# Both block compressions side by side on TensorE, the head factors between them, gate sums and first attention scores after them

## The chip, the cores and the metric

One Trainium2 chip, one core of it. The metric is the device time of one execution in microseconds (us). The kernel before takes 2090.16 us, the median of three runs (2089.99, 2090.16 and 2095.55).

## The reference: what is computed

One inference step of a decoder trunk with two layers, for a prompt of 512 tokens and for 8 sequences with 4 new tokens each (544 columns in all). Each layer has two token mixers, an mLSTM (matrix memory, 4 heads) and a sparse attention (8 query heads, 2 key heads), whose outputs are gated and merged, and then a SwiGLU channel mixer. The part that the change touches:

```
def compress(raw, pe, w1, w2):
    ...
    blocks = jnp.concatenate([ch[:, :-1], ch[:, 1:]], axis=2) + pe[None, None, :, None, :]
    hid = jax.nn.gelu(jnp.einsum('bnlgd,lde->bnge', blocks, w1))
    return jnp.einsum('bnge,ef->bngf', hid, w2)
...
kc = compress(k_cmp, pe_k, w1_k, w2_k)
vc = compress(v_cmp, pe_v, w1_v, w2_v)
...
h = h * lax.rsqrt(jnp.mean(h * h, axis=-1, keepdims=True) + EPS) * norm_g.astype(jnp.float32).reshape(M_HEADS, M_HEAD_DIM)
out = h.reshape(B, T, M_WIDTH) * jax.nn.sigmoid(o.astype(jnp.float32))
...
out = g[..., 0:1] * o_c + g[..., 1:2] * o_s + g[..., 2:3] * o_w
```

The attention has three branches: over compressed keys and values (`kc`, `vc`), over selected blocks, and over a window. Each has a softmax and a gate.

## The kernel before, in words

Each engine runs one list of instructions per layer, in the order in which its function is written (`tensor_layer`, `scalar_layer`, `vector_layer`, `gpsimd_layer`, `sync_layer`), and engines wait for one another by semaphores. No scheduler moves anything: what stands later in a function waits behind what stands earlier on that engine.

A layer goes: norm, input products, mLSTM, then the stretch of this change, then attention in 38 steps, then the large products (line 834, over half of TensorE's instructions). The stretch between mLSTM and attention, in TensorE's order:

1. `compress(0)` (lines 1178 to 1189, keys): 64 products of 64 rows by 161 columns, 16 for each of four weight units `w1`. It writes banks 0 and 6 of the result memory `ps` (`HIDDEN_BANK`). In the trace each product is two instructions, so 128.
2. The head factors (line 1203): for each of the four heads, a matrix of 4 rows spreads that head's factor over 128 partitions. The first two heads go at once. The third waits for the first one's `ha_ready`, the fourth for the second one's, since they write the same two banks. VectorE multiplies each head's output by its factor and by its sigmoid gate (lines 1812 and 1814) and signals `ha_ready`.
3. The gate sums (line 1209): the gates of the new tokens are spread into rows of `ps`. VectorE turns them into `gsel` (lines 1829 and 1830).
4. The scores of attention steps 0 and 1 (`att_scores`, line 1081), after all four `ha_ready`.
5. `compress(1)` (values), which waits for `gs_read`, VectorE's signal that the gate sums are read.
6. The second products of both compressions (lines 1222 to 1226), each behind ScalarE's `hid_ready` (GELU, lines 1510 to 1513); then ScalarE copies the compressed keys and values out (lines 1515 to 1517) and signals `cmp_ready`.
7. The scores of step 2 (line 1078), then the loop over steps: `att_turn(k)` (transposes, line 1100), the scores of step k + 3, `att_out(k)`.

ScalarE's order there is: `ha_high` of each head (line 1503, a rounding copy that is the upper half of a split; VectorE makes the lower half in line 1893), the exponentials of steps 0 and 1 (`att_exp`, line 1471), the scaling of step 0 (`att_scale`, line 1481), then both GELUs, the three copies, and the exponentials of step 2. VectorE's is: head factors, small copies of the new tokens' queries (line 1822), gate sums, masks and maxima of steps 0 and 1 (lines 1851 and 1854), weights of step 0, the four lower halves, weights of step 1 together with mask and maximum of step 2, and so on. `att_turn(1)` needs ScalarE's scaling of step 1, which comes after its exponentials of step 2.

The weight units are loaded by SyncE into a ring of four slots; a unit of `compress(1)` is loaded once the same quarter of `compress(0)` is done (`w1_used`).

Of the kernel before, what the change touches and what calls it, by code (L numbers as in the profile page):

```python
# [9 lines left out]
ALU = mybir.AluOpType  # L10
# [4 lines left out]
AX = mybir.AxisListType  # L15

P = 128
# [67 lines left out]
def columns(spec):  # L85
    at, out = 0, {}
    for name, width in spec:
# [51 lines left out]
             "cs_done": 4, "c_decayed": 4, "kw_summed": 3, "pc_done": 1, "rope_ready": 6, "hid_ready": 2,  # L139
             "cmp_done": 1, "cmp_ready": 1, "qb_ready": 1, "s_done": 38, "max_ready": 38, "exp_done": 38, "weight_ready": 30,  # L140
             "p_ready": 30, "cp_ready": 8, "t_done": 58, "t_free0": 29, "t_free1": 29, "o_done": 58, "hb_ready": 6,
             "gs_done": 1, "gs_read": 1, "merged_ready": 8, "qb_cleared": 1, "c0_landed0": 32, "c0_landed1": 32,
             "page_landed0": 64, "page_landed1": 64, "page_landed2": 64, "page_landed3": 64}

def build_step(nc, xT_in, W_in, small_in, const_in, c0_in, pages_in, table_in, win_in, cwin_in,
               y_out, fm_out, raw_out, knew_out, tm_out, u_out, pC_out, pn_out, m_out, sC_out, oldwin_out):
    with ExitStack() as ctx:
        def sb(name, shape, dt=F32):
            return ctx.enter_context(nc.sbuf_tensor(name, shape, dt))

        def sem(name):
            return ctx.enter_context(nc.semaphore(name))

        def since(layer, s, n):

            return layer * PER_LAYER[s.name] + n

        def group(layer, key):

            return layer * len(GROUPS) + GROUP[key]  # L160
# [61 lines left out]
        nstat = sb("nstat", [P, MH, 1 + DECB])  # L222
        gsel = sb("gsel", [P, 2, 3])
        gtmp = sb("gtmp", [P, 3, NH])
        hbias = sb("hbias", [P, 2])
        table = sb("table", [1, DECB * NPG], I32)
        big = slab[:, MIX_AT:SLAB_W]
# [96 lines left out]
        def bc(ap, shape):  # L324
            return ap.to_broadcast(shape)
# [95 lines left out]
        t_free = [sem(f"t_free{s}") for s in range(2)]  # L421
        o_done = sem("o_done")
        hb_ready = sem("hb_ready")
        gs_done = sem("gs_done")
        gs_read = sem("gs_read")
        merged_ready = sem("merged_ready")
        dve_step = sem("dve_step")
# [342 lines left out]
        def tensor_layer(pe, layer):  # L770
# [12 lines left out]
            def drained(q):  # L783

                for s in range(4):
                    pe.wait_ge(pair_free[s], (q - s + 3) // 4)
# [388 lines left out]
                pe.wait_ge(so_copied, since(layer, so_copied, hb + 1))  # L1175
                pe.transpose(ps[:, 7, P:2 * P], so[:, hb, :], ident).then_inc(so_turned, 1)

            def compress(v):
                for u in range(4):
                    w = landed(("w1", 4 * v + u)).rearrange("p (l e) -> p l e", e=HID)  # L1180
                    for l8 in range(8):
                        l = 8 * u + l8
                        second, l16 = divmod(l, STRIDE)
                        for g in range(NKV):

                            x = raw[g * HD:(g + 1) * HD, v, l16, second:second + NBLK + 1]
                            mm = pe.matmul(ps[:, HIDDEN_BANK[v][g], 0:NBLK + 1], w[g * HD:(g + 1) * HD, l8, :], x,  # L1187
                                           start=(l == 0), stop=(l == CLEN - 1))
                    mm.then_inc(w1_used, 1)
# [5 lines left out]
            compress(0)  # L1195
            read_out(layer, pe, ("rope", 3))
            read_out(layer, pe, ("k", 1))
            pe.wait_ge(scale_ready, since(layer, scale_ready, 1))
            for h in range(MH):
                if h >= 2:  # L1200
                    pe.wait_ge(ha_ready, since(layer, ha_ready, h - 1))
                for a in range(2):
                    mm = pe.matmul(ps[:, 2 + 2 * (h % 2) + a, 0:NHALF], sel4[0:MH, h, :], scales[:, a * NHALF:(a + 1) * NHALF],
                                   start=True, stop=True)
                mm.then_inc(scale_done, 1)
            drained(group(layer, ("ga", 0)))

            for hb in range(2):
                mm = pe.matmul(ps[:, 7, hb * 24:(hb + 1) * 24], tsel[0:NS, hb, :], gate[0:NS, TT, :], start=True, stop=True)
            mm.then_inc(gs_done, 1)  # L1210

            pe.wait_ge(rope_ready, since(layer, rope_ready, 6))
            pe.wait_ge(q_moved, since(layer, q_moved, 1))
            pe.wait_ge(ha_ready, since(layer, ha_ready, MH))
            att_scores(0)
            att_scores(1)
            pe.wait_ge(gs_read, since(layer, gs_read, 1))
            compress(1)
            w2 = sml("w2", "p (v f) -> p v f", v=2)
            pe.wait_ge(hid_ready, since(layer, hid_ready, 1))  # L1220
            for g in range(NKV):
                pe.matmul(ps[g * HD:(g + 1) * HD, 0, 0:NBLK], w2[:, 0, :], hid[:, 0, g, :], start=True, stop=True)
            pe.wait_ge(hid_ready, since(layer, hid_ready, 2))
            for g in range(NKV):
                pe.matmul(ps[0:NCP, 5, g * HD:(g + 1) * HD], hid[:, 1, g, 0:NCP], w2[:, 1, :], start=True, stop=True)
                mm = pe.matmul(ps[:, 5, P + g * HD:P + (g + 1) * HD], hid[:, 1, g, PBLK:NBLK], w2[:, 1, :], start=True, stop=True)
# [42 lines left out]
        def scalar_layer(act, layer):  # L1269
# [196 lines left out]
            def att_exp(k):  # L1466
                act.wait_ge(max_ready, since(layer, max_ready, k + 1))
                if before(k) is not None:
                    act.wait_ge(t_done, since(layer, t_done, pieces_through(before(k))))
                for r in range(parts_of(k)):  # L1470
                    ins = act.activation(part(prob(k), k, r), part(score(k), k, r), ACT.Exp, bias=stat[:, k % 3, r:r + 1],  # L1471
                                         accum_out=stat[:, 3 + k % 3, r:r + 1] if own_total(k) else None)
                ins.then_inc(exp_done, 1)
# [24 lines left out]
                            ins = act.copy(d[:, b4], o[:, b4, kv])  # L1498
                    ins.then_inc(hb_ready, 1)

            for h in range(MH):
                act.wait_ge(ha_ready, since(layer, ha_ready, h + 1))
                act.copy(ha_high[h], haT[:, h, :]).then_inc(ha_high_ready, 1)
            att_exp(0)
            att_exp(1)
            att_scale(0)

            for v in range(2):
                act.wait_ge(w1_used, since(layer, w1_used, 4 * (v + 1)))
                link(act.copy(hbias[:, v:v + 1], ps[:, HIDDEN_BANK[v][0], NBLK:NBLK + 1]))  # L1510
# [3 lines left out]
            act.wait_ge(cmp_done, since(layer, cmp_done, 1))  # L1514
            act.copy(kcT, ps[:, 0, 0:NBLK])
            act.copy(vcp[0:NCP, :], ps[0:NCP, 5, 0:P])
            act.copy(vcs, ps[:, 5, P:2 * P]).then_inc(cmp_ready, 1)

            att_exp(2)
            for k in range(NSTEP):  # L1520
# [54 lines left out]
        def vector_layer(dve, layer):  # L1575
            steps = dve_steps

            def link(ins):

                steps[0] += 1  # L1580
                ins.then_inc(dve_step, 1)
                dve.wait_ge(dve_step, steps[0])
# [225 lines left out]
            dve.wait_ge(o_gated, since(layer, o_gated, 1))  # L1808
            for h in range(MH):
                dve.wait_ge(scale_done, since(layer, scale_done, h + 1))  # L1810
                by = ps[:, 2 + 2 * (h % 2):4 + 2 * (h % 2), 0:NHALF]
                link(dve.scalar_tensor_tensor(out=halves(qm[:, h, :]), in0=halves(qm[:, h, :]), scalar=sml("mng")[:, h:h + 1], in1=by,
                                              op0=ALU.mult, op1=ALU.mult))
                dve.tensor_tensor(haT[:, h, :], haT[:, h, :], qm[:, h, :], ALU.mult).then_inc(ha_ready, 1)
# [7 lines left out]
                        ins = dve.tensor_copy(qb[g * HD:(g + 1) * HD, a, :, g * 16 + r * 4:g * 16 + r * 4 + 4],  # L1822
                                              per_seq(src[g * HD:(g + 1) * HD, r, SEQ:N]))
            ins.then_inc(qb_ready, 1)

            dve.wait_ge(gs_done, since(layer, gs_done, 1))
            for hb in range(2):
                gall = ps[:, 7, hb * 24:(hb + 1) * 24].rearrange("p (h b) -> p b h", b=3)
                link(dve.tensor_tensor(gtmp[:, :, :], gall, bc(con("rowm").unsqueeze(1), [P, 3, NH]), ALU.mult))
                ins = dve.tensor_reduce(gsel[:, hb, :], gtmp[:, :, :], AX.X, ALU.add)  # L1830
                link(ins) if hb == 0 else ins.then_inc(gs_read, 1)

            def mask_of(k):

# [52 lines left out]

            weight_and_max(None, 0)
            weight_and_max(None, 1)
            weight_and_max(0, None)  # L1890
            for h in range(MH):
                dve.wait_ge(ha_high_ready, since(layer, ha_high_ready, h + 1))
# [343 lines left out]
```

## Time and profile before

| | |
|---|---|
| median of three runs | 2090.16 us |
| the profiled execution | 2090.03 us |
| its span in the trace | 2088.4 us |
| TensorE matmul busy | 1976.9 us, 95% of the span |
| VectorE busy | 984.3 us, 47% |
| ScalarE busy | 676.0 us, 32% |
| mean granted TensorE clock | 0.952 of full speed |

Times inside the trace are us from the start of the span. The first layer's stretch starts at 273.5, the second layer's at 1305.2. A start and a duration stand ahead of each piece; "x128" is the number of instructions merged in one row. The granted clock is 1.00 for 2.4 GHz and 0.50 for 1.2 GHz; a value between is a stretch with both.

### The profile page before, as it was taken

The numbers are of one execution on the slowest core, as the hardware profiler recorded it, in microseconds if no ns is written. First come the engines' busy times: TensorE is split into PE (matmuls) and PEld (weight loads), VectorE is DVE, ScalarE is ACT, GpSimd is POOL, SyncE is SP. The second block draws the span as 40 slices with busy tenths as digits, with TensorE's granted clock in tenths as the row PEclk, the third lists the DMA queues.
The fourth block names the chain that finished last, engine by engine and source line by source line (L and its number), as shares of the span: only waits on it lengthen the run. The fifth ranks groups of instructions, "written<-read, shape, count | busy, mean of one in ns | idle before, by whom it ended". The sixth has DMA issues, their size and how long they took to land.

```text
span 2088.4 us, 34564 instructions
## 1 busy us (share of the span) xinstructions
PE 1976.9 (95%) x14490; PEld 1794.6 (86%) x14490; DVE 984.3 (47%) x1688; ACT 676.0 (32%) x1315; POOL 106.6 (5%) x148
## 2 busy tenths in 40 slices
PE   6999988889999999999989999988899999999997
PEld 5878875569999999999977878645799999999996
DVE  6343655733345442444363355666333554424434
ACT  4523236742223221222235223467322332212221
POOL 0011212000000000000001122100000000000000
PEclk9989987989999999999989899889899999999998
DMA  4202233012222223222131113520222222222221
GB/s 180 100 21 77 98 109 139 1 51 92 85 88 91 82 91 105 82 91 92 61 113 42 46 61 102 158 77 2 71 92 91 82 91 86 87 92 86 87 91 44
DMA packets 47531, 174.18 MB, mean 83 GB/s; under 512 B 6442, under 2 KB 6474, under 8 KB 46930
## 3 DMA queue, kind: packets, MB, share of 16 engines
q1 hardware_dynamic: 40178, 142.71, 21.1%
q0 software_dynamic: 7200, 29.27, 4.1%
q8 instruction: 116, 1.90, 0.4%
q14 instruction: 37, 0.30, 0.0%
HBM read 161.37 MB, written 14.71 MB: 84 GB/s over the span
## 4 chain that ended last, share of the span: by engine, by line
PE 86%; DVE 7%; ACT 5%; issue 2%; DMA 0%; DVEq 0%; SPq 0%; ACTq 0%; POOLq 0%
PE ps L834 59%; PE ps L796 3%; ACT slab L1471 2%; PE ps L1008 2%; PE ps L1187 2%; DVE stat L1854 2%; PE ps L1009 2%; PE ps L1010 2%; PE ps L872 1%; PE ps L874 1%; PE ps L873 1%; PE ps L1100 1%; PE ps L949 1%; ACT slab L1481 1%; PE ps L1081 1%
## 5 line engine op out<-in xcount | busy, mean ns | idle before, releaser
L834 PE MATMUL ps<-xh,late_w 128*128 128x272 f32 x3840 | 645.7, 289 | 1.8 <-ACT slab L1498 1.8
L834 PEld LDWEIGHTS ps<-xh,late_w 128*128 128x128 f32 x3840 | 545.1, 189 | 2.6 <-issue 2.3
L1603 DVE TENSOR_TENSOR late_w<-ring,late_w 128x1024 fp32r<-128x1024 f32 x196 | 240.2, 1225 | 645.7 <-ACT late_w L1300 645.7
L1300 ACT CAST late_w<-ring 128x1024 fp32r<-128x1024 f32 x196 | 205.3, 1048 | 716.5 <-PE ps L834 716.4
L834 PE MATMUL ps<-xl,late_w 128*128 128x272 f32 x1920 | 397.5, 289 | 0.0
L834 PEld LDWEIGHTS ps<-xl,late_w 128*128 128x128 f32 x1920 | 303.4, 190 | 0.0
L834 PE MATMUL ps<-ah,late_w 128*128 128x272 f32 x1408 | 234.7, 288 | 0.0
L834 PEld LDWEIGHTS ps<-ah,late_w 128*128 128x128 f32 x1408 | 198.7, 188 | 0.0
L1471 ACT ACTIVATE slab<-ps,stat 128x31 f32<-128x31 f32 (+5 forms) x204 | 84.4, 450 | 84.4 <-DVE stat L1854 84.4
L834 PE MATMUL ps<-mh,late_w 128*128 128x272 f32 x576 | 98.9, 288 | 0.0
L1008 PE MATMUL ps<-xh,fill_w 128*128 128x272 f32 x256 | 86.1, 336 | 0.8
L834 PEld LDWEIGHTS ps<-mh,late_w 128*128 128x128 f32 x576 | 82.3, 188 | 0.1
L1118 PEld LDWEIGHTS ps<-slab,vkv 128*64 128x64 f32 x640 | 36.2, 145 | 52.7 <-DVE slab L1905 24.9
L834 PE MATMUL ps<-al_first,late_w 128*128 128x272 f32 x384 | 79.3, 288 | 0.0
L1009 PE MATMUL ps<-xl,fill_w 128*128 128x272 f32 x256 | 78.2, 305 | 0.0
L1010 PE MATMUL ps<-xh,fill_w 128*128 128x272 f32 x256 | 77.8, 304 | 0.0
L1100 PE MATMUL ps<-const,slab 128*128 128x128 f32 (+1 forms) x384 | 62.8, 306 | 12.6 <-ACT slab L1481 12.6
L796 PE MATMUL ps<-slab,ring 128*128 128x272 f32 x256 | 63.7, 414 | 10.7 <-DVE slab L1615 10.7
L1481 ACT ACTIVATE slab<-slab,stat 128x128 f32<-128x128 f32 (+4 forms) x140 | 68.9, 558 | 10.1 <-DVE stat L1877 10.0
L796 PEld LDWEIGHTS ps<-slab,ring 128*128 128x128 f32 x256 | 51.5, 202 | 23.6 <-issue 12.2
L1100 PEld LDWEIGHTS ps<-const,slab 128*128 128x128 f32 (+1 forms) x384 | 45.2, 149 | 30.4 <-ACT slab L1481 21.5
L1118 PE MATMUL ps<-slab,vkv 128*64 128x128 f32 x640 | 54.7, 300 | 16.8 <-ACT slab L1532 9.1
(328 smaller groups left out, 2997.5 us busy)
## 6 DMA issues: line engine op xcount, KB each, us to landing
ring<-in_W SPq DMA_DIRECT2D x258, 512.0 KB, 3.5
slab<-in_pages POOLq DMA_DIRECT2D x64, 128.0 KB, 2.5
slab<-in_c POOLq DMA_DIRECT2D x8, 512.0 KB, 4.4
out_sC<-slab POOLq DMA_DIRECT2D x8, 512.0 KB, 3.1
slab<-in_win POOLq DMA_DIRECT2D x2, 2048.0 KB, 8.0
out_oldwin<-in_cwin POOLq DMA_DIRECT2D x2, 2016.0 KB, 14.1
xT<-in_xT SPq DMA_DIRECT2D x8, 272.0 KB, 4.5
out_y<-slab SPq DMA_DIRECT2D x8, 272.0 KB, 2.1
```

Of the source, the lines that this page charges most:

```text
L796: mm = pe.matmul(out[:, a, :], w[:, k, :], src[:, k, a * NHALF:(a + 1) * NHALF], start=(k == 0), stop=(k == kcs - 1))
L834: mm = pe.matmul(out[:, a, :], w[:, k * P:(k + 1) * P], x[:, a * NHALF:(a + 1) * NHALF], start=start, stop=stop)
L1008: pe.matmul(ps[:, 5, 0:NHALF], wh[:, w], xh[:, c, cols], start=(c == 0), stop=False)
L1009: pe.matmul(ps[:, 5, 0:NHALF], wh[:, w], xl[:, c, cols], start=False, stop=False)
L1010: mm = pe.matmul(ps[:, 5, 0:NHALF], wl[:, w], xh[:, c, cols], start=False, stop=(c == KC - 1))
L1100: mm = pe.transpose(ps[0:rows, 5 + x % 2, at:at + P], piece, ident)
L1118: mm = pe.matmul(ps[hd(kv), 7, r0 * P:(r0 + 1) * P], vkv[:, j, (br - 1) * P + kv * HD:(br - 1) * P + (kv + 1) * HD], PT[:, x % 2, (2 * c + ...
L1187: mm = pe.matmul(ps[:, HIDDEN_BANK[v][g], 0:NBLK + 1], w[g * HD:(g + 1) * HD, l8, :], x, start=(l == 0), stop=(l == CLEN - 1))
L1300: act.copy(hi, ring[:, u % RING, 0:hi.shape[1]]).then_inc(wh_ready, 1)
L1471: ins = act.activation(part(prob(k), k, r), part(score(k), k, r), ACT.Exp, bias=stat[:, k % 3, r:r + 1], accum_out=stat[:, 3 + k % 3, r:r ...
L1481: ins = act.activation(part(prob(k), k, r), part(prob(k), k, r), ACT.Copy, scale=stat[:, 8 + k % 3, r:r + 1])
L1603: dve.tensor_tensor(lo, ring[:, u % RING, 0:hi.shape[1]], hi.bitcast(F32), ALU.subtract).then_inc(wl_ready, 1)
```

## The change

TensorE: `compress` takes the units that it is to do. After `compress(0)` come the factors of heads 0 and 1, units 0 and 1 of `compress(1)`, the factors of heads 2 and 3, units 2 and 3 of `compress(1)`, and then the scores of steps 0 and 1. The factors use banks 1 to 4 in place of 2 to 5, since `compress(1)` writes banks 5 and 7. The gate sums move between the second products and go to unused columns of bank 5; no wait for `gs_read` is left on TensorE. ScalarE: GELUs and copies come first, with one new copy (`gall`, the gate sums, out of `ps`), then the exponentials of steps 0 and 1 and the scaling of step 0, then the four `ha_high`. VectorE: the reduction of the gate sums reads the copy and stands behind the maxima of steps 0 and 1, after `cmp_ready`.

```
-            def compress(v):
-                for u in range(4):
+            def compress(v, units=range(4)):
+                for u in units:
...
-            pe.wait_ge(scale_ready, since(layer, scale_ready, 1))
-            for h in range(MH):
+            drained(group(layer, ("ga", 0)))
+
+            def head_scales(h):
+
                 if h >= 2:
                     pe.wait_ge(ha_ready, since(layer, ha_ready, h - 1))
                 for a in range(2):
-                    mm = pe.matmul(ps[:, 2 + 2 * (h % 2) + a, 0:NHALF], ...
+                    mm = pe.matmul(ps[:, 1 + 2 * (h % 2) + a, 0:NHALF], ...
                 mm.then_inc(scale_done, 1)
-            drained(group(layer, ("ga", 0)))
-
-            for hb in range(2):
-                mm = pe.matmul(ps[:, 7, hb * 24:(hb + 1) * 24], tsel[0:NS, hb, :], gate[0:NS, TT, :], start=True, stop=True)
-            mm.then_inc(gs_done, 1)
+
+            pe.wait_ge(scale_ready, since(layer, scale_ready, 1))
+            head_scales(0)
+            head_scales(1)
+            compress(1, (0, 1))
+            head_scales(2)
+            head_scales(3)
+            compress(1, (2, 3))
...
             att_scores(0)
             att_scores(1)
-            pe.wait_ge(gs_read, since(layer, gs_read, 1))
-            compress(1)
...
             pe.wait_ge(hid_ready, since(layer, hid_ready, 2))
+            for hb in range(2):
+                pe.matmul(ps[:, 5, (2 + hb) * P:(2 + hb) * P + 24], tsel[0:NS, hb, :], gate[0:NS, TT, :], start=True, stop=True)
...
-            for h in range(MH):
-                act.wait_ge(ha_ready, since(layer, ha_ready, h + 1))
-                act.copy(ha_high[h], haT[:, h, :]).then_inc(ha_high_ready, 1)
-            att_exp(0)
-            att_exp(1)
-            att_scale(0)
-
+            act.wait_ge(ha_ready, since(layer, ha_ready, MH))
             for v in range(2):
...
             act.copy(vcp[0:NCP, :], ps[0:NCP, 5, 0:P])
+            act.copy(gall[:, :, :], ps[:, 5, 2 * P:4 * P].rearrange("p (a n) -> p a n", a=2)[:, :, 0:3 * NH])
             act.copy(vcs, ps[:, 5, P:2 * P]).then_inc(cmp_ready, 1)
+
+            att_exp(0)
+            att_exp(1)
+            att_scale(0)
+            for h in range(MH):
+                act.copy(ha_high[h], haT[:, h, :]).then_inc(ha_high_ready, 1)
...
             weight_and_max(None, 0)
             weight_and_max(None, 1)
+            dve.wait_ge(cmp_ready, since(layer, cmp_ready, 1))
+            for hb in range(2):
+                link(dve.tensor_tensor(gtmp[:, :, :], gall[:, hb, :].rearrange("p (h b) -> p b h", b=3),
+                                       bc(con("rowm").unsqueeze(1), [P, 3, NH]), ALU.mult))
...
             weight_and_max(0, None)
```

TensorE, from the first compression to the first transposes; the piece of the difference (rows count products, not the trace's instructions; L1187 is the compression in both kernels, L1203 and L1205 the head factors, L1209 and L1228 the gate sums, L1081 the first scores):

```order
 L1187 MATMUL ps<-slab,ring 128x161 x64
-L1203 MATMUL ps<-slab,const 128x272 x8
-L1209 MATMUL ps<-gate,const 128x24 x2
+L1205 MATMUL ps<-slab,const 128x272 x4
+L1187 MATMUL ps<-slab,ring 128x161 x32
+L1205 MATMUL ps<-slab,const 128x272 x4
+L1187 MATMUL ps<-slab,ring 128x161 x32
 L1081 MATMUL ps<-slab 128x256 x4
-L1187 MATMUL ps<-slab,ring 128x161 x64
-L1222 MATMUL ps<-slab,small 64x160 x2
```

The second compression now stands in two halves ahead of the scores, and nothing of VectorE's work except two heads' `ha_ready` is waited for in between.

ScalarE, the same place, before (L1503 is `ha_high`, L1471 and L1481 exponentials and scaling, L1510 and L1512 the GELU with its bias, L1515 to L1517 the copies out):

```order
L1503 CAST sq_high<-slab 128x544 x2
L1503 CAST rstd_high<-slab 128x544
L1503 CAST acc_high<-slab 128x544
L1471 ACT_TABLE_LOAD
L1471 ACTIVATE slab,stat<-ps,stat 128x128 x8
L1481 ACTIVATE slab<-slab,stat 128x128 x4
L1510 COPY hbias<-ps 128x1
L1512 ACT_TABLE_LOAD
L1512 ACTIVATE slab<-ps,hbias 128x160 x2
...
L1517 COPY slab<-ps 128x128
L1471 ACT_TABLE_LOAD
L1471 ACTIVATE slab<-ps,stat 128x31 x4
```

ScalarE in the changed kernel (L1509 and L1511 the GELU, L1514 to L1517 the copies, L1476 and L1486 exponentials and scaling, L1523 `ha_high`):

```order
L1509 COPY hbias<-ps 128x1
L1511 ACT_TABLE_LOAD
L1511 ACTIVATE slab<-ps,hbias 128x160 x2
...
L1516 COPY gall<-ps 128x48
L1517 COPY slab<-ps 128x128
L1476 ACT_TABLE_LOAD
L1476 ACTIVATE slab,stat<-ps,stat 128x128 x8
L1486 ACTIVATE slab<-slab,stat 128x128 x4
L1523 CAST sq_high<-slab 128x544 x2
L1523 CAST rstd_high<-slab 128x544
L1523 CAST acc_high<-slab 128x544
L1476 ACTIVATE slab<-ps,stat 128x31 x4
```

The eight exponentials, the four scalings and the four `ha_high` now stand between the last copy out and the exponentials of step 2 (the four of 128x31); one table load fewer is left.

## Rows read from the trace of the kernel before

**Rows 1.** The page's chain that ended last: shares of the span by line.

```profile
PE ps L834 59%; PE ps L796 3%; ACT slab L1471 2%; PE ps L1008 2%; PE ps L1187 2%; DVE stat L1854 2%; PE ps L1009 2%; PE ps L1010 2%; PE ps L872 1%; PE ps L874 1%; PE ps L873 1%; PE ps L1100 1%; PE ps L949 1%; ACT slab L1481 1%; PE ps L1081 1%
```

**Rows 2.** Chain of waits in layer 0: start, duration, engine, line, instructions.

```profile
273.50 9.05 PE ps L1187 x128
...
293.55 9.96 PE ps L1187 x128
...
304.45 0.30 PE ps L1225 x2
...
305.75 0.29 ACT slab L1515
...
307.51 0.31 DVE ps L1851
...
310.47 1.12 PE ps L1100 x4
```

**Rows 3.** Timeline between the two compressions, layer 0: start, duration, engine, line, instructions.

```profile
282.48 2.10 PE L1203 MATMUL ps<-slab,const 4*128 4x272 f32 x8
...
285.35 0.64 ACT L1503 CAST sq_high<-slab 128x544 fp32r<-128x544 f32 x1 [12.36 <-DVE slab L1814]
285.37 3.99 PE L1203 MATMUL ps<-slab,const 4*128 4x272 f32 x8 [0.79 <-DVE slab L1814]
...
288.71 1.21 PEld L1209 LDWEIGHTS ps<-gate,const 32*128 32x128 f32 x4
...
289.40 0.78 DVE L1812 SCALAR_TENSOR_TENSOR slab<-slab,small,ps 128x544 f32<-128x544 f32 x1 [0.28 <-PE ps L1203]
290.22 0.72 DVE L1814 TENSOR_TENSOR slab<-slab 128x544 f32<-128x544 f32 x1
```

**Rows 4.** Timeline from the second compression's start to the first transposes, layer 0.

```profile
294.86 0.37 ACT L1471 ACTIVATE slab<-ps,stat 128x128 f32<-128x128 f32 x1 [1.93 <-DVE stat L1854]
...
297.61 1.30 ACT L1481 ACTIVATE slab<-slab,stat 128x128 f32<-128x128 f32 x4
...
298.79 0.72 DVE L1893 TENSOR_TENSOR ha_low<-slab,acc_high 128x544 fp32r<-128x544 f32 x1
...
303.41 0.49 PE L1222 MATMUL ps<-slab,small 128*64 128x160 f32 x4
...
306.09 0.25 ACT L1517 COPY slab<-ps 128x128 f32<-128x128 f32 x1
...
306.36 1.28 ACT L1471 ACT_TABLE_LOAD   x1
...
307.99 0.70 PE L1081 MATMUL ps<-slab 64*128 64x256 f32 x4
```

**Rows 5.** Windows: stretch, length, busy PE, PEld, DVE, ACT, POOL, granted clock, DMA share, GB/s.

```profile
282.50:284.60 2.10, 2.08 (x10) 1.38 (x8) 0.79 (x2) 0.00 (x0) 0.00 (x0) 1.00 0.78 252
285.00:285.25 0.25, 0.00 (x0) 0.00 (x0) 0.25 (x2) 0.00 (x0) 0.00 (x0) 0.85 0.69 279
295.25:295.50 0.25, 0.25 (x6) 0.25 (x4) 0.22 (x2) 0.25 (x3) 0.00 (x0) 0.67 0.00 0
310.50:321.50 11.00, 11.00 (x40) 6.17 (x40) 6.57 (x21) 6.09 (x28) 4.40 (x9) 0.50 0.73 263
```

**Rows 6.** Chain of waits in layer 1: first compression, first transposes of step 1.

```profile
1305.22 9.05 PE ps L1187 x128
...
1341.15 0.90 PE ps L1100 x3
```

**Rows 7.** Timeline: the first large product after attention, layers 0 and 1.

```profile
447.43 0.79 PE L834 MATMUL ps<-xh,late_w 128*128 128x272 f32 x2 [0.91 <-ACT slab L1498]
...
1479.04 0.80 PE L834 MATMUL ps<-xh,late_w 128*128 128x272 f32 x2 [0.91 <-ACT slab L1498]
```

**Rows 8.** The second compression's loads: the timeline's row of SyncE, the page's DMA issues.

```profile
276.00 23.47 SPq L632 DMA_DIRECT2D ring<-in_W  x6
...
ring<-in_W SPq DMA_DIRECT2D x258, 512.0 KB, 3.5
```

More of the change, by code:

```diff
@@ L141 @@
              "p_ready": 30, "cp_ready": 8, "t_done": 58, "t_free0": 29, "t_free1": 29, "o_done": 58, "hb_ready": 6,
-             "gs_done": 1, "gs_read": 1, "merged_ready": 8, "qb_cleared": 1, "c0_landed0": 32, "c0_landed1": 32,
+              "gs_read": 1, "merged_ready": 8, "qb_cleared": 1, "c0_landed0": 32, "c0_landed1": 32,
              "page_landed0": 64, "page_landed1": 64, "page_landed2": 64, "page_landed3": 64}
@@ L224, in build_step @@
         gtmp = sb("gtmp", [P, 3, NH])
+        gall = sb("gall", [P, 2, 3 * NH])
         hbias = sb("hbias", [P, 2])
@@ L423, in build_step @@
         hb_ready = sem("hb_ready")
-        gs_done = sem("gs_done")
         gs_read = sem("gs_read")
@@ L1202, in tensor_layer @@
                 for a in range(2):
-                    mm = pe.matmul(ps[:, 2 + 2 * (h % 2) + a, 0:NHALF], sel4[0:MH, h, :], scales[:, a * NHALF:(a + 1) * NHALF],
+                    mm = pe.matmul(ps[:, 1 + 2 * (h % 2) + a, 0:NHALF], sel4[0:MH, h, :], scales[:, a * NHALF:(a + 1) * NHALF],
                                    start=True, stop=True)
                 mm.then_inc(scale_done, 1)
-            drained(group(layer, ("ga", 0)))
-            for hb in range(2):
-                mm = pe.matmul(ps[:, 7, hb * 24:(hb + 1) * 24], tsel[0:NS, hb, :], gate[0:NS, TT, :], start=True, stop=True)
-            mm.then_inc(gs_done, 1)
+            pe.wait_ge(scale_ready, since(layer, scale_ready, 1))
[5 more added lines that the diff above has]
+            compress(1, (2, 3))
             pe.wait_ge(rope_ready, since(layer, rope_ready, 6))
@@ L1810, in vector_layer @@
                 dve.wait_ge(scale_done, since(layer, scale_done, h + 1))
-                by = ps[:, 2 + 2 * (h % 2):4 + 2 * (h % 2), 0:NHALF]
+                by = ps[:, 1 + 2 * (h % 2):3 + 2 * (h % 2), 0:NHALF]
                 link(dve.scalar_tensor_tensor(out=halves(qm[:, h, :]), in0=halves(qm[:, h, :]), scalar=sml("mng")[:, h:h + 1], in1=by,
@@ L1824, in vector_layer @@
             ins.then_inc(qb_ready, 1)
[L1826 to L1831, printed above, removed]
             def mask_of(k):
@@ L1889, in vector_layer @@
             weight_and_max(None, 1)
+            dve.wait_ge(cmp_ready, since(layer, cmp_ready, 1))
+            for hb in range(2):
+                link(dve.tensor_tensor(gtmp[:, :, :], gall[:, hb, :].rearrange("p (h b) -> p b h", b=3),
+                                       bc(con("rowm").unsqueeze(1), [P, 3, NH]), ALU.mult))
+                ins = dve.tensor_reduce(gsel[:, hb, :], gtmp[:, :, :], AX.X, ALU.add)
+                link(ins) if hb == 0 else ins.then_inc(gs_read, 1)
             weight_and_max(0, None)
```

## The prediction

> **What bounds the kernel now.** I read the page's chain first: it is TensorE's, and most of it lies in the large products, which the change leaves alone [rows 1]. So only two stretches matter, one per layer, from the first compression to the moment at which attention runs as before. For these I read the chain of waits, then the timeline row by row, then the granted clock.
>
> The marks in layer 0 are [rows 2]: the first compression from 273.50 for 9.05 us, the second from 293.55 to 303.51, the copies out from 305.75, the mask of step 2 at 307.51, the transposes of step 1 at 310.47. I call that last moment "turn 1". From there each step of attention follows the one before as in the changed kernel, since neither the order nor the work behind it changes. So the whole change is worth the difference in the distance from the first compression's start to turn 1: 310.47 - 273.50 = 36.97 us in layer 0, and 1341.15 - 1305.22 = 35.93 us in layer 1 [rows 2, 6].
>
> Two things are to be seen. Between the compressions TensorE spends 293.55 - 282.55 = 11.0 us on little work, waiting for VectorE's head multiplications, and part of it at 1.2 GHz: eight instructions of head factors take 2.10 us, the next eight 3.99 us [rows 3]. And while the second compression runs, ScalarE does the exponentials of steps 0 and 1 (from 294.86) and the scaling (from 297.61), and VectorE ends the lower halves (298.79), all before the compression ends [rows 4]. That work is free there. The change closes the first hole and takes the cover off the second.
>
> **The new distance, part by part** (us after the first compression's start, the same for both layers).
>
> *TensorE up to the values.* Two compressions at the first one's pace: 2 x 9.05 = 18.1. Two pairs of head factors: 2.10 each in the row, including the drain of the last one [rows 3]; an estimate is 1.95 where the next matmuls follow at once, 3.9 together. Sum 22.0. No wait arises: heads 2 and 3 need heads 0 and 1 multiplied, two times 0.78 + 0.72 us [rows 3], and 4.5 us of compression lie before. The weights do not hold it up either: the first unit of the second compression is issued at 276.00 and a unit lands in 3.5 us [rows 8], while it is needed at about 284.5; the last is issued as the first compression ends and needed some 11 us later. The multiplications of heads 2 and 3 (3.0 us) and the GELU of the keys with its table load (1.28, the size of the load in [rows 4]) run beside the last 4.5 us of compression.
>
> Then the scores of steps 0 and 1: four instructions are 0.70 [rows 4], eight I put at 1.1, so 23.1. The GELU of the values ends before that: in the old kernel the first value product starts at 304.45, 0.94 after the compression's end [rows 2]. Second products of the keys 0.49 [rows 4], less drain 0.4: 23.5. The gate sums are four weight loads, 1.21 at 1.2 GHz [rows 3], so half of it, 0.6, at 2.4 GHz: 24.1. Value products, 304.45 to the copies at 305.75 [rows 2]: 1.3, so 25.4. The copies up to the end of the last one (306.09 + 0.25 = 306.34, [rows 4]) are 0.6; the new copy of the gate sums adds at most the 0.25 of that last row, I take 0.2. The compressed keys and values are ready at **26.2**. Before it was 306.34 - 273.50 = 32.84 in layer 0. Up to here the change saves 6.6 us.
>
> *From there to turn 1.* Before: 310.47 - 306.34 = 4.13. Now ScalarE has its list in front of step 2, one after another: table load 1.28, eight exponentials from 294.86 to 297.61 = 2.75, scaling 1.30 [rows 4], four upper halves at 0.64 = 2.6 [rows 3]. VectorE's last lower half follows with 0.72 [rows 4], and only then comes the mask of step 2, because weights of step 1 and mask of step 2 stand behind the lower halves in VectorE's order. From the mask to turn 1 it is 310.47 - 307.51 = 2.96 as before [rows 2]. Sum 1.28 + 2.75 + 1.30 + 2.6 + 0.72 + 2.96 = **11.6**. The scores of step 2 on TensorE and VectorE's reduction of the gate sums lie beside this list. The cover of all this was the second compression, and it is gone.
>
> *Sum.* 26.2 + 11.6 = 37.8. Against 36.97 that is +0.8 us in layer 0, against 35.93 it is +1.9 us in layer 1: +2.7 us. The profiled execution took 2090.03 us, so **2092.7 us**; that execution lies 0.1 us from the median shown. It is +0.13%, and 0.3% (6.3 us) is about what a measurement of this kernel can tell from no change.
>
> *Bounds of the unknown sizes.* Upper: head factors at 2.10, scores at twice 0.70, keys at 0.49, new copy at 0.25: +0.7 per layer. Lower: gate sums hidden in neighbouring loads (-0.6) and the scaling and halves overlapping by 0.1 per instruction of the halves (-0.4): -1.0 per layer. GpSimd's output and page loads start some 8 us earlier; I cost them at nothing, since no row here has TensorE waiting on them. After turn 1 the same instructions took 447.43 - 310.47 = 136.96 us in layer 0 and 1479.04 - 1341.15 = 137.89 in layer 1 [rows 2, 6, 7], so 0.9 per layer either way is left to chance. The forecast's own range is 2088.9 to 2095.9.
>
> **A rule against the row.** The granted clock was still 1.00 during the first pair of head factors and fell at 285.2, after TensorE had stood still for 0.79 us only [rows 3, 5]. So in this trace the head factors, four rows deep, did not hold the clock although TensorE was issuing nearly all the time. The Trainium skill, "TensorE: Matmul & The Clock Gate", section "Loop structure matters more than you think", says that matmuls which stand back to back keep the engine warm and a long wait between bursts lets it go cold. By that rule alone the new order, which has no wait between the compressions, runs at 2.4 GHz all through, and the sum is the one above. By the row the factors are weak spots, and that is the first rival.
>
> **Rivals.**
>
> *1. The clock falls inside the joined compressions (slower).* Place: the two pairs of head factors, now followed by compression in place of a wait. For it: the fall at 285.2 after just such a pair. Against it: in between now stand 4.5 us of dense work instead of waits. It decides if the granted clock shows 0.50 anywhere between the first compression and the scores. Price: the low stretch of the old kernel lasted from 285.2 to 295.4 [rows 5], 10.2 us; if all of it is TensorE's path, half of it is lost, 5.1 us. In one layer: 2092.7 + 5.1 = 2097.8; in both: 2102.9.
>
> *2. Attention starts at 2.4 GHz (faster).* In the old kernel TensorE is busy for the whole 11.00 us after turn 1, at 0.50 [rows 5]. At 1.00 half of it, 5.5 us per layer, would go: 2092.7 - 11.0 = 2081.7. Against it: in the new order TensorE has less to do before turn 1 than in the old one, for ScalarE's list is 8 us long and only the scores of steps 2 and 3 and one set of transposes lie beside it.
>
> *3. The uncovered list does not delay turn 1 (faster).* Then the distance is 26.2 + 4.13 = 30.3, a gain of 6.6 and 5.6 us: 2080.5. It needs the four halves and the eight exponentials to run while TensorE is still at the values. Both engines' orders speak against it: they stand behind the last copy.
>
> **How the numbers follow.** Forecast, within 0.3%: 0.76. Rival 1 in at least one layer: 0.15, slower. Rivals 2 and 3: 0.05 and 0.04, faster. The forecast's own range lies inside 0.3%, so the chances are 0.09, 0.76 and 0.15. The range reaches up past rival 1 in one layer, and one of the three runs shown was itself 5.4 us above the median; downwards it takes in rival 2 in one layer: 2087.0 to 2098.5.
>
> **What would show it.** Right: the second compression starts some 11 us after the first one's start and ends at about 22 us; the last copy out ends near 26.2; ScalarE then runs without a pause for about 8 us; turn 1 comes at 37 to 39 us in both layers; TensorE stands idle for several us twice in that time. Wrong: a granted clock of 0.50 between the compressions; exponentials of steps 0 and 1 ahead of the last copy; turn 1 before 35 us; or a distance from turn 1 to the first large product more than 2 us away from 137.

## The result, and the profile after

| | kernel before | changed kernel |
|---|---|---|
| median of 20 runs on one chip | 2091.44 us | 2097.33 us |
| lowest and highest of these | 2089.28 to 2095.55 | 2089.75 to 2100.86 |
| ratio, with 95% interval | | 1.0026 [1.0019, 1.0032] |
| profiled execution | 2090.03 us | 2089.75 us |
| its span | 2088.4 us | 2088.1 us |

The changed kernel is slower by 0.26%. That lies inside the 0.3% of "no change" and inside the range given (2087.0 to 2098.5), but the median is 4.6 us above the 2092.7 forecast. Of these, 1.4 come from the start of the sum: it stood on an execution of 2090.03, and the kernel before has its median at 2091.44 here. The execution that was profiled is the fastest of the 20, so this first trace shows the change at its best; a second one is among the experiments.

The chain of waits of the changed kernel in layer 0 (start, duration, engine, line, instructions) answers to [rows 2]. L1205 are the head factors, L1228 the gate sums, L1476 table load and exponentials, L1486 the scaling, L1523 and L1898 upper and lower halves, L1850 the mask:

```profile
274.19 9.05 PE ps L1187 x128
283.24 2.03 PE ps L1205 x8
285.27 4.59 PE ps L1187 x64
289.85 2.03 PE ps L1205 x8
291.88 4.59 PE ps L1187 x64
296.47 0.86 PE ps L1081 x8
...
297.75 0.55 PE ps L1228 x4
...
299.53 0.29 ACT slab L1514
...
300.06 0.16 ACT slab L1517
...
300.24 1.28 ACT L1476
...
301.53 2.91 ACT slab L1476 x16
304.44 1.15 ACT slab L1486 x4
305.59 0.54 ACT sq_high L1523
...
306.16 2.63 DVE ha_low L1898 x4
...
308.87 0.21 DVE ps L1850
```

The timeline of the same kernel, transposes of steps 0 and 1 in layer 0 and those of step 1 in layer 1 (the bracket is the wait ahead and what ended it):

```profile
305.65 1.11 PE L1100 MATMUL ps<-const,slab 128*128 128x128 f32 x4 [4.30 <-ACT slab L1486]
...
311.74 1.11 PE L1100 MATMUL ps<-const,slab 128*128 128x128 f32 x4 [0.29 <-ACT slab L1486]
...
1342.19 1.11 PE L1100 MATMUL ps<-const,slab 128*128 128x128 f32 x4 [0.29 <-ACT slab L1486]
```

Windows of the same execution (columns as in [rows 5]):

```profile
274.20:300.30 26.10, 25.32 (x297) 22.70 (x297) 15.28 (x33) 3.71 (x12) 2.22 (x2) 1.00 0.53 167
...
302.00:311.50 9.50, 3.39 (x16) 1.94 (x16) 5.42 (x17) 7.55 (x30) 3.32 (x7) 0.50 0.71 238
```

The first hole is closed: TensorE is busy for 25.32 of 26.10 us, at 2.4 GHz throughout, and the last copy out ends at 26.0 us after the first compression's start where it ended at 32.8. Behind it a new hole stands open: from 302.0 to 311.5 TensorE is busy for 3.39 of 9.50 us while ScalarE is busy for 7.55, with the list that the second compression used to cover. The first transposes wait 4.30 us for the scaling. Turn 1 comes at 311.74 - 274.19 = 37.55 us in layer 0, and the same 37.55 in layer 1, against 36.97 and 35.93 before: 0.6 and 1.6 us later.

That is 2.2 us for both layers together. The span is nevertheless 0.3 us shorter than that of the profiled execution of before, since the stretches that the change leaves alone came out 2.5 us shorter in this execution. How much such stretches move by themselves can be read from the one between the first large product of layer 0 and the first compression of layer 1, in which all kernels here do the same work: it took between 855.7 and 859.2 us in the eleven traces. So this trace confirms the mechanism and cannot by itself explain a median that is 5.9 us higher.

### The profile page after: what moved, and what is told of

Read it like the earlier page. It is cut to its first block, busy times and chain, and to the rows that moved or that the text cites. A ratio compares the mean times of both kernels' runs of the same rounds, so it can differ in the third digit from the quotient of the medians.

```text
span 2088.1 us, 34564 instructions
## 1 busy us (share of the span) xinstructions
PE 1970.8 (94%) x14490; PEld 1789.2 (86%) x14490; DVE 985.8 (47%) x1688; ACT 673.4 (32%) x1315; POOL 105.5 (5%) x148
## 4 chain that ended last, share of the span: by engine, by line
PE 85%; DVE 7%; ACT 6%; issue 2%; DMA 0%; DVEq 0%; SPq 0%; POOLq 0%; ACTq 0%
PE ps L834 59%; PE ps L796 3%; ACT slab L1476 3%; PE ps L1008 2%; DVE stat L1853 2%; PE ps L1187 2%; PE ps L1009 2%; PE ps L1010 2%; PE ps L872 1%; PE ps L874 1%; PE ps L873 1%; ACT slab L1486 1%; PE ps L949 1%; PE ps L1100 1%; PE ps L1081 1%
## 5 line engine op out<-in xcount | busy, mean ns | idle before, releaser
L1476 ACT ACTIVATE slab<-ps,stat 128x31 f32<-128x31 f32 (+5 forms) x204 | 84.6, 451 | 82.0 <-DVE stat L1853 82.0
L1118 PE MATMUL ps<-slab,vkv 128*64 128x128 f32 x640 | 56.3, 307 | 18.8 <-DVE slab L1910 10.2
L1486 ACT ACTIVATE slab<-slab,stat 128x128 f32<-128x128 f32 (+4 forms) x140 | 68.9, 559 | 9.3 <-DVE stat L1876 9.2
```

Source lines behind the costliest of these rows:

```text
L1118: mm = pe.matmul(ps[hd(kv), 7, r0 * P:(r0 + 1) * P], vkv[:, j, (br - 1) * P + kv * HD:(br - 1) * P + (kv + 1) * HD], PT[:, x % 2, (2 * c + ...
L1486: ins = act.activation(part(prob(k), k, r), part(prob(k), k, r), ACT.Copy, scale=stat[:, 8 + k % 3, r:r + 1])
```

## The experiments

For each run two distances are read from its trace: **turn 1** (from the first compression's start to the transposes of step 1), and **the rest** (from turn 1 to the first large product), in both layers. Medians and ratios come from 8 to 12 executions of each edited kernel (20 of the change in the second row) and 20 to 29 of the kernel before on the same chip. e1 to e3 share one chip, e4 to e6 another, e7 to e9 a third. The ratio is taken over all executions and is not the quotient of the two medians, so the two can differ: for e1 the medians alone would give 1.0029.

| run | turn 1, us | the rest, us | median, us | before, us | ratio [95%] |
|---|---|---|---|---|---|
| before (first trace) | 36.97, 35.93 | 136.96, 137.89 | | | |
| change (first trace) | 37.55, 37.55 | 136.57, 136.90 | 2097.33 | 2091.44 | 1.0026 [1.0019, 1.0032] |
| e1 change again | 39.22, 39.20 | 137.41, 139.42 | 2097.24 | 2091.16 | 1.0019 [1.0008, 1.0031] |
| e2 halves early | 36.36, 36.37 | 136.88, 136.71 | 2091.28 | 2091.16 | 0.9993 [0.9983, 1.0004] |
| e3 filler | 41.65, 41.64 | 133.59, 133.79 | 2094.01 | 2091.16 | 1.0011 [1.0001, 1.0020] |
| e4 one head per quarter | 39.28, 39.28 | 135.98, 138.78 | 2097.03 | 2091.92 | 1.0025 [1.0014, 1.0035] |
| e5 both edits | 36.99, 37.00 | 135.98, 136.85 | 2091.99 | 2091.92 | 1.0002 [0.9993, 1.0011] |
| e6 both edits and filler | 35.78, 38.96 | 138.36, 138.68 | 2092.49 | 2091.92 | 1.0007 [0.9998, 1.0016] |
| e7 heads early, spread | 35.49, 35.49 | 136.22, 135.85 | 2086.67 | 2090.96 | 0.9980 [0.9971, 0.9989] |
| e8 first scores under second | 38.59, 37.64 | 136.49, 137.18 | 2092.89 | 2090.96 | 1.0008 [0.9999, 1.0017] |
| e9 before, halves late | 39.05, 39.04 | 137.38, 137.43 | 2097.23 | 2090.96 | 1.0018 [1.0007, 1.0029] |

**e1: the changed kernel once more.** No edit.

> The changed kernel once more, to see in a second execution where its typical time lies, since the one profiled first (2089.75 us) was the fastest of 20. Theory A (the clock at the start of attention): median 2094 to 2099 us; the granted clock stays 1.00 from the first compression to the last copy out, turn 1 comes at 37 to 38.5 us after the first compression's start, and the loss lies behind turn 1: the distance from turn 1 to the first large product is above 138 us. Theory B (the clock falls inside the joined compressions): same median, but 0.50 between the compressions, turn 1 later than 39 us, the distance behind it 137 to 138 us.

The chain of waits of this execution, layer 0:

```profile
274.03 9.05 PE ps L1187 x128
283.07 2.02 PE ps L1205 x8
285.10 6.26 PE ps L1187 x64
291.36 2.03 PE ps L1205 x8
293.38 4.59 PE ps L1187 x64
```

Its windows at the place where the third row is longer:

```profile
284.00:285.50 1.50, 1.50 (x11) 1.03 (x11) 1.16 (x2) 0.00 (x0) 0.00 (x0) 1.00 0.84 279
285.75:286.00 0.25, 0.25 (x6) 0.25 (x4) 0.25 (x2) 0.00 (x0) 0.00 (x0) 0.60 0.26 98
286.00:289.00 3.00, 3.00 (x26) 3.00 (x24) 1.26 (x2) 0.00 (x0) 0.00 (x0) 0.50 0.06 23
289.00:289.25 0.25, 0.25 (x4) 0.25 (x4) 0.00 (x0) 0.00 (x0) 0.00 (x0) 0.58 0.00 0
```

The same 64 instructions take 6.26 us where they took 4.59. The clock falls to 1.2 GHz at 285.8, right behind the first pair of head factors, and is back at 289.2, with TensorE busy without a break before and during it. The second pair, at 291.36, does not do it. Layer 1 shows the same dip behind its first pair. It costs 1.67 us per layer: turn 1 is at 39.2 in place of 37.55. Theory B's dip and its later turn 1 are there, and the dip also shows in e2 and e3, which keep this order, in both layers; the first trace of the change has it in neither. Of theory A one layer shows its sign, a rest above 138 us (139.4; the other has 137.4): the rest is 0.8 and 2.5 us longer than in the first trace. Of the 8.0 us by which this span (2096.1) exceeds the first one, 3.3 are the two dips, 3.4 the rest in two layers, and 1.3 other stretches. Time goes with the clock in the 20 executions of the change as well: the seven with a mean granted clock of 0.951 or 0.952 took 2089.8 to 2095.3 us, the eight at 0.948, which is e1's, 2095.9 to 2099.5. So e1 is the more typical of the two traces.

**e2: halves early.** ScalarE's upper halves and VectorE's lower halves go back under the second compression (ScalarE's edit is shown, VectorE's is the same move):

```
+            for h in range(MH):
+                act.wait_ge(ha_ready, since(layer, ha_ready, h + 1))
+                act.copy(ha_high[h], haT[:, h, :]).then_inc(ha_high_ready, 1)
             for v in range(2):
...
             att_scale(0)
-            for h in range(MH):
-                act.copy(ha_high[h], haT[:, h, :]).then_inc(ha_high_ready, 1)
```

> Only the upper and lower halves of the heads' outputs go back ahead of the GELUs and of the gate sums, under the second compression. If ScalarE's list behind the last copy sets turn 1, the four upper halves (2.6 us), the last lower half (0.7) and the part of the scaling beside VectorE's work leave the path: turn 1 at 33 to 35 us instead of 37.6, 3 to 4 us less per layer, 2088 to 2092 us where the changed kernel takes 2097. If the list is not on the path: no difference to the changed kernel. Theory A adds that the shorter wait of TensorE also saves clock, so 2086 to 2090; theory B has the clock loss of the compressions left in, 2090 to 2093.

The timeline of this run, transposes of steps 0 and 1 in layer 0:

```profile
307.27 1.12 PE L1100 MATMUL ps<-const,slab 128*128 128x128 f32 x4 [4.22 <-ACT slab L1486]
310.52 1.12 PE L1100 MATMUL ps<-const,slab 128*128 128x128 f32 x4
```

3.25 us from the transposes of step 0 to those of step 1, where the change has 6.1. Turn 1 is 36.4 with the dip still in it, 2.8 us earlier than e1's; that is above the 33 to 35 expected, and without the dip's 1.67 it would be 34.7. The median falls by 6.0 us against e1, of which turn 1 in two layers is 5.7, and the kernel is as fast as before: 0.9993 [0.9983, 1.0004]. The list was on the path, and without the halves in it the rest of the change is worth nothing measurable.

**e3: filler.** 14 products of no use behind the scores of step 2 and 6 behind those of step 3, to keep TensorE busy:

```
+                    pe.matmul(ps[:, 6, 0:NHALF], ones[:, :], cos[:, 0:NHALF], start=True, stop=True)
...
+            warm(14)
             for k in range(NSTEP):
...
+                if k == 0:
+                    warm(6)
```

> The changed kernel with 14 products of no use (128x272, written to bank 6) behind the scores of step 2 and 6 more behind those of step 3, where TensorE only waits. Theory A: the granted clock stays 1.00 up to turn 1 and for a part of the steps behind it, 2 to 5 us less per layer: 2087 to 2093 us. Theory B: no difference to the changed kernel, 2095 to 2099. If the products stand in the way of the transposes, slower than the changed kernel by up to 3 us per layer.

Its windows in layer 0, from the first filler to 11 us behind turn 1 (316.06):

```profile
303.30:306.70 3.40, 3.40 (x8) 2.56 (x9) 0.51 (x3) 3.39 (x19) 0.16 (x1) 0.50 0.47 74
306.70:311.00 4.30, 4.30 (x20) 3.54 (x20) 2.94 (x7) 2.93 (x7) 2.00 (x4) 1.00 0.79 259
316.00:327.00 11.00, 8.59 (x60) 4.76 (x56) 7.92 (x22) 5.85 (x28) 5.89 (x12) 1.00 0.41 118
```

The clock fell as the filler began, so this ran at 1.2 GHz first and delayed turn 1 to 41.65. From 306.7 on the clock was 1.00 and stayed so over the first 11 us of attention, and the rest took 133.6 and 133.8 us, 3.8 and 5.6 less than e1's. That is not yet what the clock is worth: turn 1 came 2.4 us later than in e1, and the other engines went on meanwhile (VectorE has 227 instructions left in the rest of layer 0, against 232 in e1). Turn 1 and the rest together are 175.2 and 175.4 us, against 176.6 and 178.6 in e1 and 174.1 and 174.5 in the first trace of the change. The median, 2094.0, lies between the two expectations; it is 3.2 us below e1's, but the intervals of the two ratios overlap, so a gain is not shown.

**e4: one head per quarter.** In place of two heads per half:

```
-            head_scales(0)
-            head_scales(1)
-            compress(1, (0, 1))
-            head_scales(2)
-            head_scales(3)
-            compress(1, (2, 3))
+            for h in range(MH):
+                head_scales(h)
+                compress(1, (h,))
```

> The changed kernel with one head's factors ahead of each quarter of the second compression, in place of two heads ahead of each half. In the second execution of the changed kernel (and in two other runs with the same order) the granted clock fell for 3.4 us behind the first pair of factors, and the two compressions with their factors took 23.9 us in place of 22.3. If it is the pair of factors in one piece that drops the clock, it stays 1.00 up to the last copy out, the compressions take 22.3 us and turn 1 comes at 37.6 in both layers; 3.3 us less in an execution that had the dip twice: median 2093 to 2096. If four rows of factors drop it however they are spread, no difference: 2096 to 2099.

No dip in either layer. But turn 1 stays at 39.28, and the time at 2097.03. ScalarE's timeline, layer 0 (L1506 and L1508 the GELU with its bias and table load, L1511 the first copy out):

```profile
296.83 0.16 ACT L1506 COPY hbias<-ps 128x1 f32<-128x1 f32 x1 [22.80 <-DVE slab L1817]
297.01 1.28 ACT L1508 ACT_TABLE_LOAD   x1
298.30 0.68 ACT L1508 ACTIVATE slab<-ps,hbias 128x160 f32<-128x160 f32 x2
...
301.64 0.29 ACT L1511 COPY slab<-ps 128x160 f32<-128x160 f32 x1 [1.90 <-PE ps L1228]
```

The last head's factors come late, the GELU of the keys waits for VectorE's last multiplication until 296.83, 22.3 us after the first compression's start where the change had 294.02 (19.8), and the copies are at 301.64 (27.1, not 25.3). Four single heads also cost more than two pairs: the two compressions with factors take 23.1 us, not the 22.3 expected. What the clock gave, these two took. The first half of the expectation held, the second did not.

**e5: both edits together.** e2's and e4's, no other line.

> Both edits: halves ahead of the GELUs, one head's factors ahead of each quarter. If both causes are right and add up: compressions 22.3 us, turn 1 at 34.7, median 2086 to 2090, faster than the kernel before by 0.1 to 0.2%. If the dip is not mended by the spreading: as with the halves alone, 2090 to 2092.

A miss: turn 1 at 37.0, 2091.99. Again no dip, but the two gains do not add up, for the reason that e4 shows: the last head's multiplication and its upper half now stand ahead of the GELU of the keys, and the copies start at 27.6 us.

**e6: both edits and a short filler.** `warm(3)` ahead of the wait for the copies, `warm(8)` behind the scores of step 2.

> The run with both edits, and 3 products of no use ahead of the wait for the copies and 8 behind the scores of step 2, few enough not to delay the transposes at 1.2 GHz (8 x 0.45 = 3.6 us in a wait of 4.2). In the run with 20 such products the distance from turn 1 to the first large product fell from 137 to 139 us to 133.7. If that came from the clock at the start of attention, the same here: 2 to 4 us less per layer than without, 2080 to 2086. If it only came from the later turn 1, no difference to the run with both edits.

A miss as well: 2092.49. In layer 0 the filler ran at 1.00 and turn 1 came at 35.78; in layer 1 it came at 38.96. Windows, layer 1 (turn 1 is at 1344.70):

```profile
1333.70:1340.40 6.70, 6.70 (x19) 4.98 (x18) 3.37 (x15) 6.67 (x30) 1.62 (x3) 0.50 0.64 111
1340.50:1350.50 10.00, 7.56 (x55) 5.33 (x53) 5.84 (x16) 2.63 (x13) 4.30 (x9) 1.00 0.75 288
```

There most of the filler ran at 1.2 GHz and stood in the way. The expectation had also put it too short: a product is two instructions in the trace, and the eight products took 3.9 us at 2.4 GHz in layer 0 and 5.3 us at mixed clock in layer 1, not 3.6 at 1.2 GHz. What matters more is the rest. In both layers the clock was 1.00 at turn 1 and for some 6 us behind it (to 1350.5 here), and still the rest took 138.4 and 138.7 us, where e5, with 0.50 at turn 1, took 136.0 and 136.9. So the clock at the start of attention, by itself, gave nothing here, and e3's shorter rest can't be put down to it.

**e7: halves early, heads early and spread.** e2, and the heads one by one from the middle of the first compression on:

```
+            compress(0, (0, 1))
...
+            head_scales(0)
+            compress(0, (2,))
+            head_scales(1)
+            compress(0, (3,))
+            head_scales(2)
+            compress(1, (0,))
+            head_scales(3)
+            compress(1, (1, 2, 3))
```

> Halves ahead of the GELUs as before, and the four heads' factors one by one earlier: ahead of the third and fourth quarter of the first compression and of the first and second quarter of the second. The spread run lost behind the compressions what it saved in the dip, since the last head came late and with it the GELU of the keys. If that is so: no 0.50 between the compressions, both compressions with factors 22.3 to 23.1 us, turn 1 at 34.5 to 35.5 us in both layers, 1 to 2 us less per layer than with the halves alone: 2087 to 2090. If the lateness of the GELU was not it, turn 1 stays at 36.4 to 37 and the time at 2091 to 2092.

TensorE's timeline, layer 0:

```profile
273.85 4.66 PE L1187 MATMUL ps<-slab,ring 64*128 64x161 f32 x64 [1.69 <-DVE slab L1777]
278.44 1.18 PE L1205 MATMUL ps<-slab,const 4*128 4x272 f32 x4
279.55 2.46 PE L1187 MATMUL ps<-slab,ring 64*128 64x161 f32 x32
...
288.96 1.18 PE L1205 MATMUL ps<-slab,const 4*128 4x272 f32 x4
290.06 6.85 PE L1187 MATMUL ps<-slab,ring 64*128 64x161 f32 x96
...
309.34 1.12 PE L1100 MATMUL ps<-const,slab 128*128 128x128 f32 x4
```

No dip, the last head is done at 290, and turn 1 comes at 35.49 in both layers. 2086.67 us, ratio 0.9980 [0.9971, 0.9989]: faster than the kernel before, and by about 10 us than the change, 0.3 us below the range expected. Turn 1 is 0.87 us earlier than in e2: the dip's 1.67 is gone, and 0.8 is paid for four single heads (the compressions with factors take 23.1 us). In two layers that is 1.8 of the 4.6 us between the medians of e2 and e7; the rest of the gain is not placed, and the two were measured on different chips.

**e8: first scores under the second compression.** e7, with `att_scores(0)` and `att_scores(1)` ahead of the last two quarters, and the exponentials between the two GELUs (VectorE's weights of step 0 move ahead of its wait for the copies, not shown):

```
+            compress(1, (1,))
...
             att_scores(1)
+            compress(1, (2, 3))
...
+            gelus(0)
+            att_exp(0)
+            att_exp(1)
+            att_scale(0)
+            gelus(1)
```

> As the run with early spread factors, but the scores of steps 0 and 1 go ahead of the last two quarters of the second compression and ScalarE does the exponentials of both steps and the scaling between the two GELUs, so that they are covered again, at the price of two more table loads (1.28 each). If the uncovered exponentials are the rest of the loss: turn 1 at 32.5 to 34.5 us, 2083 to 2088. If the table loads and the later GELU of the values take it back: turn 1 at 35 or later, no difference to the run with early spread factors.

The price won. ScalarE's timeline, layer 0 (L1489 the scaling, L1514 and L1516 the GELU of the values, L1525 the first copy out):

```profile
299.80 1.28 ACT L1489 ACTIVATE slab<-slab,stat 128x128 f32<-128x128 f32 x4 [1.56 <-DVE stat L1881]
300.98 0.14 ACT L1514 COPY hbias<-ps 128x1 f32<-128x1 f32 x1
301.14 1.28 ACT L1516 ACT_TABLE_LOAD   x1
302.43 0.68 ACT L1516 ACTIVATE slab<-ps,hbias 128x160 f32<-128x160 f32 x2
306.19 0.29 ACT L1525 COPY slab<-ps 128x160 f32<-128x160 f32 x1 [3.08 <-PE ps L1234]
```

The scaling waits 1.56 us for VectorE, whose four lower halves (295.70 to 298.32) stand there ahead of the sums of step 0 that the scaling needs; the expectation had no such term. The table is loaded again behind it, and the GELU of the values ends at 303.1, 5.7 us after the compressions' end. The copies start at 32.75 us, 0.5 later than in the kernel before (32.25). Turn 1 is beyond 35 as this branch said, but the time is not that of e7: it is 6 us longer. What this order would give with the lower halves placed later was not run.

**e9: the kernel before with the halves late.** The mirror of e2:

```
-            for h in range(MH):
-                act.wait_ge(ha_ready, since(layer, ha_ready, h + 1))
-                act.copy(ha_high[h], haT[:, h, :]).then_inc(ha_high_ready, 1)
             att_exp(0)
...
+            for h in range(MH):
+                act.wait_ge(ha_ready, since(layer, ha_ready, h + 1))
+                act.copy(ha_high[h], haT[:, h, :]).then_inc(ha_high_ready, 1)
             att_exp(2)
```

> The kernel before with only the four upper halves moved behind the copies out (the lower halves wait for them as ever). If halves behind the copies delay the mask of step 2: four casts of 0.55 to 0.65 us and the last lower half lie between the copies and the mask, where 1.2 us stood: turn 1 1.7 to 2.3 us later in each layer, 2094 to 2097. If turn 1 does not hang on them: no difference, 2091 to 2092.

The chain of waits of this run, layer 0 (L1514 the last copy out, L1851 the mask of step 2):

```profile
307.01 0.16 ACT slab L1514
307.17 0.55 ACT sq_high L1518
...
307.75 2.63 DVE ha_low L1893 x4
...
310.46 0.21 DVE ps L1851
```

First upper half and four lower halves lie between copies and mask, 3.2 us. Turn 1 is at 39.05 and 39.04, 2.1 and 3.1 us later than in the first trace of the kernel before, and the median is 2097.23 against 2090.96; layer 1 and the median go slightly beyond what was expected. By the medians (+6.3 us) this one block, moved alone, costs the kernel before about as much as the whole change did (+5.9); by the ratios it is 1.0018 [1.0007, 1.0029] against 1.0026 [1.0019, 1.0032], which overlap.

## Why the prediction was right, and which size was off

- *Distance up to the last copy out: 26.2 forecast, 26.0 measured.* Compressions with head factors 22.28 (22.0 said), the scores 0.86 (1.1), gate sums 0.55 (0.6). No wait arose and no load was late.
- *From there to turn 1: 11.6 forecast, 11.5 measured.* Table load 1.28, exponentials 2.91, scaling 1.15, halves 0.54 + 0.03 + 2.63 = 3.2, mask to turn 1 2.87. The pace of the halves is VectorE's, not ScalarE's as I had put it; the sum is the same. e2 and e9 show by taking the block out and by putting it in that these instructions are on the path.
- *Turn 1: 37.8 forecast, 37.55 measured in both layers*, so +2.2 us where +2.7 stood.
- *Rival 1, the clock inside the joined compressions, with a chance of 0.15: this is the step that was mis-sized, twice.* It shows in both layers of e1, e2 and e3 and in neither layer of the first trace, so in three of four traces with this order: the chance was too low. Its price is 1.67 us per layer, not the 5.1 taken from the kernel before: there the clock stayed low for 10.2 us, with waits in between, here for 3.4 us, with dense compression. The way to the price was right (half of the low stretch, and half of 3.4 is 1.7); the length of the stretch was not. The old one was an upper bound, and I used it as the size.
- *The clock behind turn 1* was given 0.9 us per layer either way. e1 has 0.5 and 1.5 us more there than the kernel before had in its trace, 2.0 in both layers.
- *Signs, and luck.* The first trace of the change shows all that the prediction named as signs of being right. e1, the more typical one, shows two that it named as signs of being wrong: 0.50 between the compressions, and in layer 1 a rest of 139.4 us, more than 2 from 137; its turn 1 of 39.2 lies outside 37 to 39. That the median still falls within 0.3% (5.9 of 6.3 us) is in part luck: the dip came more often than was said and cost a third of what was said.
- *Median +5.9 where +2.7 stood.* Against the trace of before, e1 gives turn 1 2.2 + 3.3 us later (list and two dips) and a rest 2.0 us longer: 7.5. The change's first trace gives 2.2 and a shorter rest. The median lies between. How often each pattern occurs over executions can't be read from one trace per run, and what decides between them is left open.
- *Rivals 2 and 3* did not come: attention starts at 0.50, and the list stands behind the copies. The price of rival 2, 5.5 us per layer, is not borne out: e6 had the clock at 1.00 at turn 1 in both layers, and its rest was not shorter. The time given for rival 3 is also wrong as a sum: a gain of 6.6 and 5.6 us goes off the 2090.0 of the kernel before, not off the forecast, which gives 2077.8 and not 2080.5.
- *The rule against the row.* By the rule alone (the Trainium skill, "TensorE: Matmul & The Clock Gate", section "Loop structure matters more than you think") the joined compressions stay at 2.4 GHz. The first trace agrees with it, 1.00 over 26.1 us; e1 does not: 0.50 from 285.8 to 289.2 with TensorE busy all the time. The measurement decides: in e1 the clock fell although the products stood back to back, with the head factors in between.

## What to carry to other kernels

When work is pulled together on the engine that bounds the kernel, list what the other engines did under the old gap and under the work that moved: here, in layer 0, the copies came 6.8 us earlier and 7.4 us of ScalarE's and VectorE's work were uncovered. A block that nobody needs for 100 us (the halves, first read at 462 us) goes where an engine waits anyhow, never at the head of a serial chain; that one placement was the difference between the change and no change (e2), and together with earlier and spread head factors it made the same idea a gain of 0.2% (e7).

## What the runs showed of the hardware that was not expected

Products of 4 rows by 272 columns, 2.0 us of them in one piece between dense compressions, were followed by a fall of the granted clock to 1.2 GHz in six of eight layers traced, without any idle time of TensorE from the start of the first compression on. Cut into four pieces of 1.1 us with at least 2.4 us of compression between them they never were, in the ten layers of e4 to e8. These are four traces against five, and the six falls were all on the chip of e1 to e3, where no spread run was traced; so that the piece's length is the cause is likely, not shown. Against the chip as the cause stands that the same pair, followed by waits, had the clock fall in both layers of e9, on the chip of e7 and e8. And a filler meant to hold the clock can start too late: in e3 and in layer 1 of e6 part of it ran at half speed and delayed what it should have sped up, and where it did hold the clock up to turn 1, in both layers of e6, the rest of attention was no shorter.
